# Rows picked straight from x, the norm's factor in the pick matrix, one ring place moved and tile 0 routed ahead

## What is computed

```python
x = x + merged @ w_out[l]
h2 = rms_norm(x, norm_ffn[l])
x = x + hier_moe(h2, w_router_group[l], b_router_group[l], w_router_expert[l], b_router_expert[l],
                 w_expert_gate[l], w_expert_up[l], w_expert_down[l])

# hier_moe: a token goes to the 2 best of 8 experts of the best of 4 groups
return (jax.nn.silu(xb @ w_g[e]) * (xb @ w_u[e])) @ w_d[e]      # an expert, w_g and w_u 1024x512, w_d 512x1024
```

## Time and profile before

| | us |
|---|---|
| three runs | 701.58, 702.25, 702.77 |
| median | 702.25 |
| the profiled execution | 701.26 |
| its span | 699.1 |
| PE busy | 615.8 (88%) |
| DVE busy | 279.8 (40%) |
| ACT busy | 199.6 (29%) |
| POOL busy | 28.5 (4%) |

### The profile page before, as it was taken

How to read it: one execution, slowest core, us unless ns; L and a number is a source line. 1 busy time by engine, 2 the same in 40 slices (tenths; PEclk the granted TensorE clock), 3 DMA queues, 4 the chain that set the end, 5 groups by cost and what they waited for, 6 DMA issues and landing times.

```text
span 699.1 us, 11551 instructions
## 1 busy us (share of the span) xinstructions
PE 615.8 (88%) x4690; PEld 373.8 (53%) x4690; DVE 279.8 (40%) x623; ACT 199.6 (29%) x334; POOL 28.5 (4%) x54
## 2 busy tenths in 40 slices
PE   8999999999999998999987788775878857797876
PEld 5887899999999893333332233322323323332333
DVE  6476976985474945333231112211112211120311
ACT  5684455473535433121111111111111111110111
POOL 2612000000000020000000000000000000000000
PEclk9999999999999999999997989999889998887999
DMA  9995347436479799999999999999999999999995
GB/s 314 309 373 185 133 139 221 155 133 229 166 272 420 304 387 398 428 424 426 429 426 427 429 427 427 427 425 427 428 427 429 425 428 427 428 425 429 426 419 211
DMA packets 40388, 247.53 MB, mean 354 GB/s; under 512 B 4456, under 2 KB 6640, under 8 KB 26128
## 3 DMA queue, kind: packets, MB, share of 16 engines
q1 hardware_dynamic: 37872, 245.44, 86.6%
q0 software_dynamic: 912, 1.25, 1.0%
q10 hardware_dynamic: 1552, 0.10, 0.2%
HBM read 245.72 MB, written 1.06 MB: 353 GB/s over the span
## 4 chain that ended last, share of the span: by engine, by line
PE 57%; DMA 40%; DVE 1%; issue 1%; SPq 0%; POOL 0%; POOLq 0%; DVEq 0%
DMA wide<-in_w_expert_up 35%; PE ps L1431 9%; PE ps L1048 6%; PE ps L1049 6%; PE ps L1050 6%; DMA wide<-in_w_expert_down 5%; PE ps L1468 3%; PE ps L1023 3%; PE ps L1025 3%; PE ps L1024 3%; PE ps L1442 2%; PE ps L1524 2%; PE ps L1079 2%; PE ps L1395 1%; PE ps L1404 1%; PE ps L1091 1%
## 5 line engine op out<-in xcount | busy, mean ns | idle before, releaser
L1431 PE MATMUL ps<-wide,xe 128*32 128x512 f32 x1024 | 147.5, 700 | 72.0 <-DMA wide<-in_w_expert_up 70.2
L2083 DVE TENSOR_TENSOR he<-g_s,ps 128x128 f32<-128x128 f32 x32 | 9.2, 289 | 267.1 <-ACT g_s L935 264.2
L1431 PEld LDWEIGHTS ps<-wide,xe 128*32 128x32 f32 x1024 | 31.2, 119 | 145.0 <-issue 128.8
L1603 DVE TENSOR_TENSOR ring_lo<-ring,w_hi 128x1024 fp32r<-128x1024 f32 x76 | 91.3, 1222 | 41.4 <-ACT w_hi L742 41.0
L742 ACT ACTIVATE w_hi<-ring 128x1024 fp32r<-128x1024 f32 x76 | 78.9, 1057 | 54.8 <-PE ps L1050 34.9
L935 ACT ACTIVATE g_s<-ps 128x128 f32<-128x128 f32 x32 | 8.9, 277 | 252.1 <-PE ps L1442 252.1
L1048 PE MATMUL ps<-hT_hi,w_hi 128*128 128x256 f32 x288 | 80.4, 279 | 0.0
L1049 PE MATMUL ps<-hT_lo,w_hi 128*128 128x256 f32 x288 | 79.5, 276 | 0.0
L1050 PE MATMUL ps<-hT_hi,ring_lo 128*128 128x256 f32 x288 | 79.5, 276 | 0.0
L1524 PE MATMUL ps<-y,back 64*128 64x512 f32 x240 | 59.6, 611 | 1.9 <-ACT y L943 0.9
L1468 PE MATMUL ps<-wide,he 128*32 128x512 f32 x472 | 56.8, 598 | 0.0
(11 more groups left out here) (288 smaller groups left out, 790.9 us busy)
## 6 DMA issues: line engine op xcount, KB each, us to landing
wide<-in_w_expert_gate SPq DMA_DIRECT2D x27, 2048.0 KB, 46.8
wide<-in_w_expert_up SPq DMA_DIRECT2D x27, 2048.0 KB, 48.9
wide<-in_w_expert_down SPq DMA_DIRECT2D x26, 2048.0 KB, 42.5
ring<-in_w_in SPq DMA_DIRECT2D x8, 2048.0 KB, 14.7
ring<-in_w_merge_gate SPq DMA_DIRECT2D x6, 2048.0 KB, 8.7
wide<-in_w_expert_gate SPq DMA_DIRECT2D x10, 1024.0 KB, 9.4
wide<-in_w_expert_up SPq DMA_DIRECT2D x10, 1024.0 KB, 13.5
wide<-in_w_expert_down SPq DMA_DIRECT2D x10, 1024.0 KB, 10.1
```

The source lines that it names most:

```text
L1431: ins = t_.matmul(ps[q * WIN:(q + 1) * WIN, b, :], xe[b][:, j % 2, 2 * c + j // 2, :], w[:, C * j:C * (j + 1)], start=(c == 0 and j < 2), ...
L1603: v.tensor_tensor(piece(ring_lo, g, c), piece(ring, g, c), by_row(out_hi[g == 19][c]).bitcast(F32), ALU.subtract).then_inc(wpre_lo, 1)
```

## The change

- `scr`, `w_al`, `zT` and `reset` now stand side by side in 8 KB per partition and become place 20; `x_tok` keeps its own memory and is no place of the ring. Load 20 waits for `halves_squared`, a signal that DVE gives after the two half sums of squares, and is issued right after load 16.
- The copies `xn2` are gone. `pick_rows` reads `x_tok`: a quarter of the output is the columns 2q and 2q + 1 of every eight. The factor of the norm (`rstd`) is multiplied into `pick_w`; for that `join` adds the two halves of `same` in a step of its own. ACT's copy of the picked rows puts the columns in order.
- On PE the low-order part of the last quarter is a function of its own, the last transposes of tile 0 stand in its middle, and tile 0's last router product comes ahead of most of the last quarter. DVE finishes tile 0 before the last addition of tile 1. The compare `eh` comes after the first `pick_w`.
- The number of passes is read before expert 8 (`COUNT_AT`), not 1.
- `fin`, the staging of the output, is `x_tok`.

```diff
+COUNT_AT = 8
...
-                elif n != 20:
+                elif n == 20:
+                    sp.wait_ge(halves_squared, 1)
+                else:
                     sp.wait_ge(proj_done, first_bank[NPRE - 2] + 6)
-                else:
-                    sp.wait_ge(seeded, 1)
-                    sp.wait_ge(xn0_ready, 1)
-                    sp.wait_ge(xn1_ready, 1)
                 load(n)
...
-            for n in [0, 1, 2, 3, 11] + list(range(4, 11)) + [12, 14, 13, 15, 16, 18, 17, 19, 21, EXTRA, 20]:
+            for n in [0, 1, 2, 3, 11] + list(range(4, 11)) + [12, 14, 13, 15, 16, 20, 18, 17, 19, 21, EXTRA]:
...
-                s_.activation(xr[:, :], bank(e % 2)[:, 0:QW], ACT.Copy).then_inc(rows_out, 1)
+                s_.activation(xr[:, :].rearrange("p (k f) -> p k f", k=2), bank(e % 2)[:, 0:QW].rearrange("p (f k) -> p k f", k=2),
+                              ACT.Copy).then_inc(rows_out, 1)
...
-            out_quarter(1, 1, range(0, 2))
+            out_quarter_low(1, 1, range(0, 4))
+            turn_x1(0, range(6, KD), 5)
+            out_quarter_low(1, 1, range(4, KD))
             turn_x1(1, range(4, 6), 4)
-            turn_x1(0, range(6, KD), 5)
-            out_quarter(1, 1, range(2, 5))
-            route(0, range(6, KD), 5)
-            out_quarter(1, 1, range(5, KD))
-            route(1, range(4, 6), 4)
+            out_quarter(1, 1, range(0, 1))
+            route(0, range(6, KD), 4)
+            out_quarter(1, 1, range(1, KD))
+            route(1, range(4, 6), 5)
...
-                        ins = t_.matmul(ps[q * WIN:(q + 1) * WIN, e % 2, 0:QW], pick_w[e % 2][:, tt, :], xn2[tt][:, QW * q:QW * (q + 1)],
+                        rows_q = x_tok[:, tt, :].rearrange("p (f k) -> p f k", k=KD)[:, :, 2 * q:2 * q + 2]
+                        out_q = ps[q * WIN:(q + 1) * WIN, e % 2, 0:QW].rearrange("p (f k) -> p f k", k=2)
+                        ins = t_.matmul(out_q, pick_w[e % 2][:, tt, :], rows_q,
                                         start=(tt == 0), stop=(tt == TT - 1))
...
             group_of(0)
+            in_group(0)
+            best_two(0)
             x1_add(1, 2)
             square_sum(1, 2)
             mean_square(1)
-            in_group(0)
             scale_out(1)
-            best_two(0)
             group_of(1)
...
+            def join():
+
+                return v.tensor_tensor(same[:, :, 0, :], same[:, :, 0, :], same[:, :, 1, :], ALU.add)
+
             def one_row(dst):
 
-                return v.tensor_tensor(dst[:, :, :], same[:, :, 0, :], same[:, :, 1, :], ALU.add)
+                return v.tensor_tensor(dst[:, :, :], same[:, :, 0, :], rstd, ALU.mult)
```

More of the change, by code:

```diff
@@ L141, in hybrid_block @@
         w_hi = [place(f"w_hi{c}", [P, CW], F32R) for c in range(CHUNKS)]
-        x_at = top[0]
+        scr_at = top[0]
+        scr = place("scr", [P, 2, C], F32)
+        w_al_at = top[0]
+        w_al = place("w_al", [P, 256], F32)
+        zT = place("zT", [P, T], F32)
+        top[0] += 1024
+        reset = place("reset", [P, T], F32)
+        xn_at = top[0]
+        assert xn_at - scr_at == 4 * UNIT
+        xn = place("xn_merged", [P, TT, D], F32)
         x_tok = place("x_tok", [P, TT, D], F32)
-        xn_at = top[0]
-        xn = place("xn_merged", [P, TT, D], F32)
         merged_lo = place("merged_lo", [P, KD, T], F32R, at=xn_at)
@@ L158, in hybrid_block @@
         on_w = place("on_w", [P, 1], F32)
[L159 to L164, removed]
         table = place("table", [BUCKETS, NH], F32)
         w_r_at = top[0]
+        assert w_r_at - vectors_at == 8 * WIN
         w_r = place("w_r", [P, KD, NLOG], F32)
@@ L258, in hybrid_block @@
         probT = aqk[:, 1, :, :].rearrange("p a b -> p (a b)")[:, 0:768].rearrange("p (a b) -> p a b", a=2)
[L261 to L264, removed]
+        fin = [x_tok[:, tt, :] for tt in range(TT)]
+        squares = [place("squares_half", [P, C], F32, at=scr_at)]
+        squares += [place("squares_quarter", [P, QW], F32, at=late_at)] * 2
         here_at = [h2T_at]
@@ L1268, in out_half, with low_row, out_begin, out_quarter_low @@
                     ins.then_inc(chunk_done, 1)
-            def out_quarter(tt, q, ks=range(KD)):
[L1272 to L1277, removed]
+            def low_row(q, k):
+                return ring_lo[19 % PRE_RING][:, UNIT * q + QW * k:UNIT * q + QW * (k + 1)]
+            def out_begin(tt, q):
+                r = first_bank[19] + tt
+                if q == 0:
+                    pe.wait_ge(evacuated[r % 4], r // 4)
+                else:
+                    pe.wait_ge(x1_ready, tt + 1)
+            def out_quarter_low(tt, q, ks=range(KD)):
+                if ks[0] == 0:
+                    out_begin(tt, q)
+                for k in ks:
+                    ins = t_.matmul(bank(2 * q + tt)[:, 0:QW], merged_hi[:, k, tt * P:(tt + 1) * P], low_row(q, k),
+                                    start=(k == 0), stop=False)
+                if ks[-1] == KD - 1:
+                    ins.then_inc(chunk_done, 1)
+            def out_quarter(tt, q, ks=range(KD)):
+                if tt == 0 and ks[0] == 0:
+                    out_begin(tt, q)
                 rows = slice(tt * P, (tt + 1) * P)
                 o = bank(2 * q + tt)[:, 0:QW]
[L1280 to L1284, removed]
                 for k in ks:
@@ L1291, in out_quarter @@
                     if tt == 0:
-                        t_.matmul(o, merged_hi[:, k, rows], wl[k], start=False, stop=False)
+                        t_.matmul(o, merged_hi[:, k, rows], low_row(q, k), start=False, stop=False)
                     ins = t_.matmul(o, merged_lo[:, k, rows], wh, start=False, stop=(k == KD - 1))
```

68 lines of the change are left out of this document (35 added, 33 removed).

## The result

| | before | after |
|---|---|---|
| median of 22 runs each, us | 701.66 (700.03 to 702.77) | 703.12 (701.90 to 704.04) |
| ratio | | 1.0019, 95% interval 1.0013 to 1.0025 |
| profiled execution, us | 701.26 | 701.90 |
| its span, us | 699.1 | 699.9 |

The forecast was 701.6 us with a range of 700.2 to 702.9. The kernel became 1.5 us slower and lies above the range. The forecast stood on the median of three runs, 702.25 us; 22 runs of the same kernel gave 701.66. From that base the same gain of 0.65 us would have read 701.0, so the change was missed by 2.1 us and not by 1.5.

A forecast was written before the change was run, and what follows sets the result against it. Expert-weight transfers at 427 GB/s bound it; only holes matter. Load 23 issued at 268.7 us lands at 276.45 instead of 277.1; pick and other edits +0: 702.25 - 0.65 = 701.6 us, range 700.2 to 702.9.

The forecast's parts named there:

- What bounds the kernel: Weight transfers to the end, 427 GB/s from 280 us; only holes in the stream count, 2.8 us in all.
- All else in the stream shifting with it: Everything in the stream of transfers was to shift with load 23's landing, 0.65 us earlier.
- signs of being right: Load 20 issued near 247.8, no dip at 256 to 262, one hole before 23, pick 1.07 us, expert 1's idle mostly gone.
- signs of being wrong: Load 23 issued before 268 us, pick over 1.2 us, or stream off 427 GB/s in 280 to 600 us.
- Load 20 and the holes: Load 20 issued behind 16 at about 247.8 us; holes at 257 and 268 go, a new one stands before 23.
- The size of the gain: 0.65 us: Load 23 lands at 276.45 us against 277.1 before, so 0.65 us gained.
- the first rival (no new hole): Load 23 issued by 267.95 us or its transfer starting sooner; 1.4 to 2.3 us gained, 700.0 to 700.85 us; chance 0.18.
- The routing chain: Steps from tile 0's last router product to load 23's issue; 0.1 us gained, 23 issued at 268.7 us.
- The strided pick: PE's pick reading column pairs straight from x_tok; 16 records stay at 1.07 us, +0.
- both bounds (+1.1 and +2.9): Dearer pick: +1.1 us by ACT's stride ratio, +2.9 us if column groups lose their overlap; slow-pick rival's chance 0.12.
- Edits worth nothing: Strided copy of picked rows, join's extra DVE step, later pass count (at most 1.68 us of PE's wait): 0 us.

The follow-up runs named there:

- e1: Kernel before with scr placed ahead of x_tok, so everything from x_tok on moves up 4096 bytes; 704.28 us, ratio 1.0044 to before.
- e5: Kernel after with yc_hi alone moved up by 2496 bytes, to 64 above a multiple of 256; 700.09 us, ratio 0.9973 to before.
- h1: Kernel after with its map moved: loaded operands at a multiple of 256, streamed ones 192 above; 697.15 us, ratio 0.9936 to before.
- h3: Kernel before with its whole memory map moved up by 128 bytes and nothing else; 699.05 us, ratio 0.9959 to before.
- f1: Kernel of e5 with load 20 issued last again, behind the extra place; 701.46 us, ratio 0.9999 to before.
- f3: Kernel of e5 with the old routing order of the kernel before on PE, ACT and DVE; 700.24 us, ratio 0.9979 to before.
- f2: Kernel of e5 with the number of passes read before expert 1 again; 700.00 us, ratio 0.9978 to before.

## Why the prediction was wrong, step by step

**What bounds the kernel** was right: 426 to 427 GB/s from 280 us on before and after, and only holes and shifts of the stream moved the end.

**"All else in the stream shifting with it"** is the step that failed. The prediction costed the region from the merge on and took everything ahead of it as unchanged, because PE's instructions there are the same. The moved addresses had no line in the sum: not a row, not a bound, not a rival. They cost 2.9 us by the spacing, 2.5 to 2.6 by medians (e1: +2.5 with addresses alone; e5 against the kernel after: -2.6). Two of its signs of being right gave it away, load 20 issued near 247.8 us and 23 at 268.5 to 268.9 (250.24 and 271.20 came); none of its signs of being wrong asked whether the stretch ahead of the merge had kept its length.

**Load 20 and the holes.** Issued 0.4 us behind 16 as said (247.70 less the shift), no hole at 256 to 262, one hole in front of 23. e5 is 0.41 us late from its first stage; less that, X landed at 270.5 us against 270.8 worked out, and 23 at 276.55 against 276.45.

**The size of the gain: 0.65 us** was the second error, a term too small by a factor of more than two. It was 1.7 us (e5 against before) to 1.9 (h1 against h3). What was off is the landing of 23 in the kernel *before*: worked out as 277.1 us (20's landing plus 4.91 us), when it was 268.82 + 9.6 = 278.4. The row was there to be read. So were the bytes: the earlier trace rows had holes of 1.5 and 0.8 us going and one of 0.75 coming, which is 1.55 us. Landings of load 23 in before, of f1, and of e5:

```profile
wide<-in_w_expert_gate SPq DMA_DIRECT2D x1, 2048.0 KB, 9.6
```

```profile
wide<-in_w_expert_gate SPq DMA_DIRECT2D x1, 2048.0 KB, 9.5
```

```profile
wide<-in_w_expert_gate SPq DMA_DIRECT2D x1, 2048.0 KB, 7.9
```

In f1 as in before, load 20 is still under way when 23 is issued, and 23 lands 5.9 to 6.2 us behind it, not 4.91 (5.7 in the second profile of before, 5.1 in h3, so one profile's figure is loose by an us). A model of one server at 427 GB/s misses this. By the bytes moved in the 52.7 us from the issue of 16 on, e5 is 1.3 us ahead of before's first profile and 1.8 ahead of its second, against 1.9 by the landings; a byte count is a mean over 16 DMA engines, a landing is the slowest of them. That the engines were out of step after a hole is my reading and was not measured.
Load 23 in e5, into a queue that has all but run out, took 7.9 us, 3.0 of them beyond its bytes. By the 0.6 us of the Trainium skill (DMA: Bandwidth & Descriptors, section "Specifications") it would have been 5.5, by estimate; the trace stays with the figure read from the earlier trace rows, and the first rival (no new hole) did not come.

**The routing chain** went step by step: tile 0's logits 256.96 (257.1 worked out), tile 1's addition 258.72 (258.84), tile 1's logits 260.86 (260.85), 23's issue 268.66 (268.7). 0.1 us was said, 0.17 measured by f3.

**The strided pick**: 16 records in 1.13 us against 1.07, 6% dearer; "+0" was right within 0.1, both bounds (+1.1 and +2.9) are out. The Trainium skill (SBUF — State Buffer, section "Door 1: The DMA port swizzle", note on cachelines) has a pair of fp32 in a 16-byte line read at full rate; the trace agrees but for these 0.06 us.

**Edits worth nothing**: the pass count was (f2). But the 1.68 us of idle time before expert 1 in the earlier trace rows was not its doing: it is 0.52 us after and 0.52 in f2 as well. What took it away was, by the rows, another edit, which the diff above leaves out: in the kernel before, PE also waits for `fold_ready` ahead of expert 1's first product, in the kernel after behind it. In the trace of before `fold` (L2068) ends last, behind `npass` (L2058) and `xe` (L2040), and PE starts at 273.36 us:

```profile
270.26 0.14 DVE L2058 CAST npass<-cntr 1x1 int32<-1x1 f32 x1
271.72 0.42 DVE L2040 TENSOR_TENSOR xe<-ps,g_ffn 128x256 f32<-128x256 f32 x1 [0.65 <-PE ps L1404]
272.38 0.23 DVE L2068 TENSOR_TENSOR fold<-ident 128x64 f32<-128x64 f32 x1
```

No run undid that edit alone.

The sum with the measured terms: -1.7 to -1.9 for the ring, +2.5 to +2.9 for the map, which is +0.6 to +1.2; the medians gave +1.46 and, on the second occasion, +0.94. Of the +1.46, 0.3 us or more has no term.

## What to carry over

A memory map is an edit of its own: when tiles move, give the moved addresses a line in the sum, and look in the trace at the spacing of the same matmuls ahead of the change before looking at the change. If PE is busy without a break and does fewer matmuls in a window at the same clock, try another offset of one operand, which is one number in one line; here a map 128 bytes higher, with one operand set to fit, took 5.5 us off the kernel after (702.70 to 697.15), about three times what the change itself is worth. When a transfer meets others in the queue, read its landing in the trace of before; don't derive it. If landings and bytes give different sizes for a hole, as 0.65 and 1.55 us here, carry both into the range.

## What the runs showed of the hardware

- Products of 128x256 with fp32r operands follow each other every 113.4, 117.8 or 120.0 ns at a granted clock of 1.00. The offsets of the loaded and the streamed operand in 256 bytes set which: 113.4 with the streamed one 64 bytes below the loaded one, at three pairs of places. A distance of 128 was not tried; the reason is not known.
- A row without a break can keep its spacing past the operand that caused it: the 576 matmuls behind the 96 that stream `yc` stayed at 117.8 ns, though `hT` stood well. Rows with good offsets can also start slow: that of 96 at 10.6 us was at 117.8 ns in all four profiles of the kernel before and its variants, and at either spacing in those of the kernel after. What picks it is open.
- The five short rows (11 to 24 matmuls) behind 242 us stood at 117 to 120 ns in every profile. They load `merged` and stream the weights; no distance tried made them fast.
- The stream of weights ran 0.6% faster (430 against 427 GB/s, 2.5 us over 380 us) with the whole map 128 bytes higher; with its first byte at 64 or 192 above a multiple of 256 it stayed at 427.
- In e5's profiled execution PE stood for 2.38 us before the last gate and up product, and from 680.49 us on the granted clock was at the lower of its two levels (1.2 GHz) for 3.41 us: the product took 3.62 us instead of 1.92. In the second profile of the kernel after it took 2.96 us behind 1.81 us of idle time, in the first 1.92. This makes single executions of one kernel differ by a microsecond. Standing alone does not decide it: in h3 1.64 us of idle time were followed by 1.92 us at the full clock.

```profile
680.45 3.62 PE L1439 MATMUL ps<-wide,xe 128*32 128x512 f32 x16 [2.38 <-DMA wide<-in_w_expert_up]
```
